# Experts' weights read in longer runs, the router tile by tile, and the first group of tokens gathered by a product

## The chip, the cores and the metric

One core of a Trainium2 chip runs the whole program. Its engines are TensorE (PE; its weight loads are PEld), VectorE (DVE), ScalarE (ACT), GpSimd (POOL) and SyncE (SP), and sixteen DMA engines move data. The metric is the device time of one execution in microseconds. All arithmetic is in f32.

## The reference

Three layers over 256 tokens of 1024 features. The first block has two (a gated-scan mixer and windowed attention, each followed by an MLP); the second block has one layer that ends in a mixture of experts, which is where most of the change lies:

```python
x = x + g1[:, None, :] * mix
h2 = _rms(x, norm2_g[l]) * (1.0 + sc2[:, None, :]) + sh2[:, None, :]
g_logits = hf @ w_rg + b_rg                      # 4 groups
e_logits = (hf @ w_re + b_re).reshape(-1, 4, 4)  # 16 experts
...                                              # best group, its best 2 experts, softmax weights
for e in range(N_EXPERTS):                       # 16 experts, 1024 -> 512 -> 1024
    he = jax.nn.silu(hf @ w1[e]) * (hf @ w3[e])
    y = y + combine[:, e:e + 1] * (he @ w2[e])
x = x + g2[:, None, :] * y
```

Each of the 256 tokens takes two experts, so 512 pairs are spread over 16 experts, unevenly.

## The kernel before

Each engine has an order of its own, written out by hand, and semaphores join them. SP issues all large weight loads in one fixed order. PSUM has eight banks; PE takes them in turn (`claim`) and other engines free them (`free`, `moved`).

The expert stage works on slots. Every expert has 64 slots (`SLOTS`); seven more units of 64 slots (`SPILLS`) take what overflows. So there are 23 units, in the order of `moe_order`: experts 0, 1, spill unit 0, experts 2, 3, spill unit 1, and so on to 12, 13, spill unit 6, 14, 15. Two units' slots make a group of 128 rows; there are 12 groups. A spill unit is computed whether or not it is needed, but its weights are loaded only where a table, made at run time, says that an expert overflowed.

What leads to the first unit, in order:

- DVE adds the last output projection to the residual, normalises both tiles of tokens (`rms_row`), PE transposes them (`turn_x("moe", ...)`), ACT and DVE apply scale and shift (`modulate`), PE makes the gate rows and the router's product for both tiles, and DVE picks experts with small operations.
- PE's product `pos` counts tokens per expert; DVE turns the counts into slots (`slot_i`, `slots_ready`).
- POOL scatters the token rows to their slots in DRAM (`x_slots`, four indirect DMAs, `x_spread`), loads the first group of 128 rows back (`load_group`), PE transposes it (`turn_group`), and ACT and DVE apply scale and shift (`modulate_group`, `hs_ready`).
- Meanwhile DVE makes `pick_late`, one-hot weights with which the last two units' results are added to tokens by PE instead of through DRAM; PE transposes them (`turn_picks`).

Then each unit is `up(i)`: 16 products of 64 slots by 512 columns of w1 and w3, in two pairs of 64 columns of the array, with `turn_he(i-1)` in their middle; `turn_group` where a group begins; and `down(i-1)`: 8 products with w2. ACT makes the silu and DVE the gated product `he`. DVE scales the result (`keep_y`) and POOL stores it to `y_slots`, from which four indirect loads at the end collect each token's two rows.

SP's order for the expert weights (`load_up`: w1 and w3, 2 MB each; `load_down`: w2, 2 MB): experts 0 and 1, spill unit 0 (after the table and the scatter, since its buffer lies over the token rows), then 2, 3 and so on. Two experts' buffers alternate, so `load_up(e)` waits until expert e-2 is through `up`. w1 and w3 are read as `(k p) n -> p k n`: partition p takes row k*128+p of each of 8 blocks, 2 KB at a time; w2's rows are 4 KB.

GpSimd's queue also carries, at the start of the second block, small loads (`rel_bias`, norm vectors, router weights `wr`), and inverse square roots for DVE (`inverse_roots`).

## Time and profile before

| | us |
|---|---|
| median of three runs (1716.3 to 1721.85) | 1717.02 |
| the profiled execution's own time | 1726.32 |
| its span, first to last instruction | 1724.5 |
| TensorE busy in the span (94%) | 1626.6 |
| VectorE busy (40%) | 697.5 |
| ScalarE busy (15%), GpSimd busy (6%) | 256.0, 108.3 |
| DMA moved in the span | 333.94 MB |

Read it as a stage at a time: a share over the whole span averages stages with different limits. The profiled execution took 9.3 us more than the median; sums below are made against the profiled one. "Issue" in the chain is time in which an engine waited for nothing that the profile can name, a weight load among it. A matmul in f32 shows as two records, a transpose as one. The DMA share can read over 1, since packets overlap.

### The profile page before, as it was taken

What the parts mean: (1) busy time and instruction counts of PE and PEld (TensorE: products, weight loads), DVE (VectorE), ACT (ScalarE), POOL (GpSimd) and SP (SyncE); (2) the same over time, 40 slices, a digit from 0 to 9 for tenths busy, and PEclk for the clock granted to TensorE, in tenths of its full rate; (3) what the DMA queues carried; (4) which work ended last, traced back from release to release, by engine and by line L of the source; (5) the groups of instructions that cost most, each with busy time, mean ns of one, the idle gap of its engine ahead of it and who ended that gap; (6) DMA issues with size and microseconds to landing.
All of it is one profiled execution on the core that took longest, in us unless ns stands there. A gap on an engine that the chain in (4) does not pass through costs nothing.

```text
span 1724.5 us, 17356 instructions
## 1 busy us (share of the span) xinstructions
PE 1626.6 (94%) x6960; PEld 878.5 (51%) x6960; DVE 697.5 (40%) x1322; ACT 256.0 (15%) x576; POOL 108.3 (6%) x123
## 2 busy tenths in 40 slices
PE   4999999999999999999989999999989958998997
PEld 2445556474444444446756788448855633333332
DVE  1617853468886000112264765004484342111112
ACT  3121113010000000000154110000222311011110
POOL 1000001100000000001000100001131110110101
PEclk9999999999999999999989999999999978999999
DMA  9452441146665321107610699424623449999996
GB/s 340 169 195 99 146 165 56 49 147 219 214 225 207 135 98 49 49 1 257 225 50 1 229 333 363 175 98 154 197 98 122 147 178 354 390 392 391 391 387 254
DMA packets 160623, 333.94 MB, mean 194 GB/s; under 512 B 15288, under 2 KB 15568, under 8 KB 160544
## 3 DMA queue, kind: packets, MB, share of 16 engines
q1 hardware_dynamic: 141408, 298.90, 47.7%
q0 software_dynamic: 18224, 30.78, 5.5%
q10 hardware_dynamic: 912, 3.17, 0.5%
q8 instruction: 55, 0.90, 0.2%
q14 instruction: 24, 0.20, 0.0%
HBM read 355.02 MB, written 15.48 MB: 215 GB/s over the span
## 4 chain that ended last, share of the span: by engine, by line
PE 88%; DMA 4%; DVE 4%; issue 2%; POOL 1%; ACT 1%; SPq 0%; DVEq 0%; ACTq 0%; POOLq 0%
PE psum L624 85%; PE psum L628 4%; DMA wring<-in_ev_w_in 2%; DMA wring<-in_w_mod 1%; DMA wring<-in_mlp_w 1%; ACT wide L1663 0%; POOL small L1523 0%; DVE wide L2068 0%; DVE big L2401 0%; DMA x_slots<-wide,slot_i 0%; DVE big L2560 0%; DMA big<-x_slots 0%; DVE small L2559 0%; POOL x_slots L1609 0%; DVE small L2183 0%
## 5 line engine op out<-in xcount | busy, mean ns | idle before, releaser
L624 PE MATMUL psum<-wring,big 128*128 128x512 f32 (+2 forms) x1600 | 559.6, 579 | 13.8 <-issue 13.3
L624 PE MATMUL psum<-wide,wring 128*128 128x256 f32 (+3 forms) x1872 | 490.2, 437 | 0.2
L624 PEld LDWEIGHTS psum<-wring,big 128*128 128x128 f32 (+1 forms) x1600 | 242.8, 173 | 310.1 <-issue 306.1
L624 PEld LDWEIGHTS psum<-wide,wring 128*128 128x128 f32 (+1 forms) x1872 | 304.3, 184 | 173.0 <-issue 144.6
L624 PE MATMUL psum<-wring,wide 128*128 128x512 f32 (+3 forms) x576 | 216.1, 576 | 9.0 <-DMA wring<-in_w_mod 5.4
L1663 ACT ACTIVATE big<-psum 128x512 f32<-128x512 f32 (+2 forms) x155 | 83.0, 546 | 665.0 <-PE psum L624 614.3
L2068 DVE SCALAR_TENSOR_TENSOR wide<-wring,csilu,wide 128x512 f32<-128x512 f32 x252 | 175.5, 748 | 3.0
L624 PEld LDWEIGHTS psum<-wring,wide 128*128 128x128 f32 (+1 forms) x576 | 97.7, 188 | 109.2 <-issue 96.0
L2168 DVE TENSOR_TENSOR wide<-psum,gate 128x512 f32<-128x512 f32 x27 | 18.7, 691 | 325.2 <-PE psum L624 325.0
L1523 POOL TENSOR_TENSOR small<-small 128x1 f32<-128x1 f32 (+2 forms) x30 | 41.1, 1372 | 1037.8 <-DVE small L2185 884.7
L1663 ACT ACTIVATE wide<-psum 128x256 f32<-128x256 f32 (+2 forms) x114 | 46.0, 418 | 313.3 <-PE psum L628 158.9
L624 PE MATMUL psum<-big,wide 128*64 128x512 f32 (+1 forms) x408 | 90.7, 566 | 0.0
L2836 DVE TENSOR_TENSOR wide<-wide,psum 128x256 f32<-128x256 f32 x23 | 9.7, 421 | 179.0 <-ACT wide L1663 179.0
L2068 DVE SCALAR_TENSOR_TENSOR big<-wring,csilu,big 128x512 f32<-128x512 f32 x112 | 74.9, 745 | 0.0
L2216 DVE TENSOR_TENSOR big<-big,psum 128x512 f32<-128x512 f32 (+1 forms) x62 | 35.1, 567 | 97.3 <-ACT big L1663 94.3
L1663 ACT ACTIVATE wide<-psum,modc 128x256 f32<-128x256 f32 (+1 forms) x36 | 16.2, 514 | 348.8 <-PE psum L628 348.6
L624 PE MATMUL psum<-big 128*64 128x128 f32 (+5 forms) x592 | 59.3, 328 | 7.7 <-ACT wide L1663 3.6
L624 PEld LDWEIGHTS psum<-big,wide 128*64 128x64 f32 (+1 forms) x408 | 30.8, 142 | 49.2 <-issue 48.3
L624 PE MATMUL psum<-wide,lnb 128*64 128x512 f32 x224 | 50.8, 595 | 0.0
L624 PEld LDWEIGHTS psum<-big 64*128 64x128 f32 (+2 forms) x592 | 41.6, 168 | 17.1 <-issue 15.6
L628 PEld LDWEIGHTS psum<-const,wide 128*128 128x128 f32 x214 | 24.9, 150 | 37.9 <-issue 25.5
L628 PE MATMUL psum<-const,wide 128*128 128x128 f32 x214 | 35.3, 300 | 5.6 <-DVE wide L2208 4.8
(266 smaller groups left out, 885.5 us busy)
## 6 DMA issues: line engine op xcount, KB each, us to landing
wring<-in_mlp_w SPq DMA_DIRECT2D x32, 2048.0 KB, 8.7
wring<-in_w SPq DMA_DIRECT2D x32, 2048.0 KB, 21.9
wring<-in_w_mod SPq DMA_DIRECT2D x24, 2048.0 KB, 13.0
big<-in_w SPq DMA_DIRECT2D x23, 2048.0 KB, 20.6
wide<-in_w SPq DMA_DIRECT2D x14, 2048.0 KB
wring<-in_w_ada SPq DMA_DIRECT2D x12, 2048.0 KB, 8.6
wring<-in_w_in SPq DMA_DIRECT2D x8, 2048.0 KB, 8.4
wring<-in_ev_w_in SPq DMA_DIRECT2D x6, 2048.0 KB, 13.0
```

The lines of the kernel that those rows point to most:

```text
L624: return nc.tensor.matmul(o, a, b, start=first, stop=last)
L628: return nc.tensor.transpose(o, a, ident[0:n, 0:n])
L1523: nc.gpsimd.tensor_tensor(a, a, half_neg[:, 0:a.shape[1]], ALU.pow).then_inc(rate_done, 1)
L1663: return nc.scalar.activation(o, a, func, **kw)
L2068: ins = v_.scalar_tensor_tensor(acc, w, by, acc, ALU.mult, ALU.add)
L2168: free(v_.tensor_tensor(ubuf, bank(name), gate[:, gv, cs], ALU.mult), name)
L2216: free(v_.tensor_tensor(h, h, src, ALU.mult), name)
L2836: v_.tensor_tensor(he[:, i % 2, :], sg[:, i % 2, :], psum[:, i % 2, T:2 * T], ALU.mult).then_inc(he_ready, 1)
```

## The change

Four parts.

1. The experts' matrices are read with each partition taking neighbouring rows. w1 and w3 are read as `(p k) n -> p k n`: partition p takes rows 8p to 8p+7, one run of 16 KB. w2 is read as two halves of which partition p takes two neighbouring rows, runs of 8 KB. The inner dimension of a product is then dealt otherwise over partitions, so the token rows (`rms_row(t, True)`), the router's weights, the scale and shift (`modp`) and `he` are dealt the same way. `modp` comes from `modc` by way of DRAM: two stores of 1024 single numbers and one load, all in POOL's queue.
2. The router runs tile by tile: transposes, scale and shift, and product of tile 0 stand inside and right behind the output projection of tile 1. The gate rows come after both products.
3. The first group isn't read back from DRAM: DVE makes a one-hot matrix from the slots (`first_hot`) and PE multiplies the token rows with it (`gather_first`), which gives the transposed group. The scatter stays, for the other eleven groups.
4. `turn_picks` comes after `up(0)`, and the work of DVE and ACT around it is put in another order. The loads of spill unit 0 also wait for the gather.

On PE, from the second tile's output projection to the second unit, this stands in a row before (`small,wide` is the router, `const,modc` the gate rows, `lnb,const` the counting, `const,gate` the picks, `const,big` the group's transposes, `wring,big 64x512` an `up`):

```order
L624 MATMUL psum<-wring,big 128x512 x24
L628 MATMUL psum<-const,wide 128x128 x16
L624 MATMUL psum<-const,modc 128x128 x8
L624 MATMUL psum<-small,wide 128x20 x16
L624 MATMUL psum<-lnb,const 128x32 x2
L628 MATMUL psum<-const,gate 128x128 x4
L628 MATMUL psum<-const,big 128x128 x8
L624 MATMUL psum<-wring,big 64x512 x24
L628 MATMUL psum<-const,wide 128x128 x2
```

and now:

```order
L642 MATMUL psum<-wring,big 128x512 x16
L646 MATMUL psum<-const,wide 128x128 x8
L642 MATMUL psum<-wring,big 128x512 x8
L642 MATMUL psum<-small,wide 128x20 x8
L646 MATMUL psum<-const,wide 128x128 x8
L642 MATMUL psum<-small,wide 128x20 x8
L642 MATMUL psum<-const,modc 128x128 x8
L642 MATMUL psum<-lnb,const 128x32 x2
L642 MATMUL psum<-lnb,wide 128x128 x16
L642 MATMUL psum<-wring,big 64x512 x16
L646 MATMUL psum<-const,gate 128x128 x4
L642 MATMUL psum<-wring,big 64x512 x8
```

The router's product is in two halves, the first of them right behind the output projection; the gate rows have moved behind both; the group's eight transposes are sixteen products `lnb,wide`; and the picks stand behind the first unit.

On DVE, from the slots to the first unit (`table_i` says which spill units are needed, `modc` or `modp` marks the scale and shift of a group, `64x512` begins the picks), before:

```order
L2784 CAST slot_i<-lnb 128x4
L2787 TENSOR_TENSOR lnb<-lnb,const 128x112
...
L2793 CAST table_i<-lnb 128x14
L2796 TENSOR_TENSOR small<-small 128x2x4
L2797 TENSOR_TENSOR small<-small 128x2
...
L2804 TENSOR_TENSOR small<-small 128x2
L2809 COPY gate<-gate 64x512 x2
L2814 TENSOR_SCALAR wide<-const,lnb,small 128x128
...
L2823 TENSOR_SCALAR big<-psum,modc 128x128 x4
L2836 TENSOR_TENSOR wide<-wide,psum 128x256 x2
```

and now:

```order
L2841 CAST slot_i<-lnb 128x4
L2842 TENSOR_SCALAR small<-lnb 128x4
L2844 TENSOR_SCALAR lnb<-const,small 128x128 x2
L2846 SCALAR_TENSOR_TENSOR lnb<-const,small,lnb 128x128 x2
L2851 TENSOR_TENSOR lnb<-lnb,const 128x112
...
L2857 CAST table_i<-lnb 128x14
L2862 TENSOR_SCALAR big<-psum,modp 128x128 x4
L2868 TENSOR_REDUCE small<-small 128x2
...
L2878 COPY gate<-gate 64x512 x2
L2883 TENSOR_SCALAR lnb<-const,lnb,small 128x128
...
L2897 TENSOR_TENSOR wide<-wide,psum 128x256 x2
```

Five operations for `first_hot` stand between the slots and the table; the group's scale and shift have moved ahead of the picks.

The diff, without the declarations and the places that repeat an edit shown:

```diff
--- before.py
+++ after.py
...
@@ -444,0 +449 @@
+        modp_scratch = nc.dram_tensor("modp_scratch", [2, D], F32, kind="Internal").ap()
...
@@ -592 +600,11 @@
-                 "moe": (2, 1, 0, 0, 2, 4)}
+                 "moea": (2, 1, 0, 0, 1, 4), "moeb": (2, 1, 0, P, 1, 4)}
+
+        def shift_of(part, k):
+
+            l, half, v = PARTS[part][:3]
+            return modp[:, 0, k:k + 1] if (l, half) == (2, 1) else modc[:, l, 24 * half + k, v:v + 1]
+
+        def scale_of(part, k):
+
+            l, half, v = PARTS[part][:3]
+            return modp[:, 1, k:k + 1] if (l, half) == (2, 1) else modc[:, l, 24 * half + 8 + k, v:v + 1]
@@ -1294,2 +1312 @@
-            out_project(2, yT2, (2,), turn_second)
-            out_project(2, yT2, (3,))
+            def turn_routed(part, t):
@@ -1297,6 +1314,7 @@
-            pe.wait_ge(xn_ready, 4)
-            turn_x("moe", xn, (0, 1))
-            gate_rows(2, 1)
-            wait_h("moe")
-            o = claim("router")
-            for t in range(2):
+                pe.wait_ge(xn_ready, 3 + t)
+                turn_x(part, xn, (t,))
+
+            def router(part, t):
+
+                wait_h(part)
+                o = claim(f"router{t}")
@@ -1304,2 +1322,9 @@
-                    last = mm(o[:, t * 20:(t + 1) * 20], hT[:, k, t * P:(t + 1) * P], wr[:, k, :], k == 0, k == KC - 1)
-            last.then_inc(bank_full, 1)
+                    last = mm(o[:, 0:20], hT[:, k, t * P:(t + 1) * P], wr[:, k, :], k == 0, k == KC - 1)
+                last.then_inc(bank_full, 1)
+
+            out_project(2, yT2, (2,), turn_second)
+            out_project(2, yT2, (3,), lambda: turn_routed("moea", 0))
+            router("moea", 0)
+            turn_routed("moeb", 1)
+            router("moeb", 1)
+            gate_rows(2, 1)
@@ -1318,3 +1343,2 @@
-                pe.wait_ge(xs_in[n % 2], 16 * (n // 2 + 1))
-                if n > 0:
-                    pe.wait_ge(hs_ready, 2 * n)
+                pe.wait_ge(xs_in[n % 2], 16 * (n // 2 + n % 2))
+                pe.wait_ge(hs_ready, 2 * n)
@@ -1324,0 +1349,9 @@
+            def gather_first():
+
+                pe.wait_ge(first_ready, 1)
+                for k in range(KC):
+                    for t in range(2):
+                        last = mm(psum[:, 4 + k // 4, (k % 4) * P:(k % 4 + 1) * P], xn[:, t, k * P:(k + 1) * P],
+                                  first_hot[:, t, :], t == 0, t == 1)
+                last.then_inc(xs_turned, 1)
+
@@ -1388,3 +1421 @@
-            turn_picks()
-            turn_group(GROUP_ORDER[0])
-            pe.wait_ge(late_ready, 1)
+            gather_first()
@@ -1392,0 +1424,4 @@
+                if i == 0:
+                    turn_picks()
+                if i == 2:
+                    pe.wait_ge(late_ready, 1)
@@ -1441,0 +1477,4 @@
+            def by_halves(w):
+
+                return w.rearrange("p (h c) n -> p h c n", h=2)
+
@@ -1449 +1488 @@
-                    sp.dma_start(w13_ring[e % 2][:, w], src[0, e].rearrange("(k p) n -> p k n", p=P)).then_inc(w13_in[e % 2], 16)
+                    sp.dma_start(w13_ring[e % 2][:, w], src[0, e].rearrange("(p k) n -> p k n", p=P)).then_inc(w13_in[e % 2], 16)
@@ -1456 +1495 @@
-                sp.dma_start(w2_ring[:, e % 2], I["w2_2"][0, e].rearrange("(f p) n -> p f n", p=P)).then_inc(w2_in[e % 2], 16)
+                sp.dma_start(by_halves(w2_ring[:, e % 2]), I["w2_2"][0, e].rearrange("(h p c) n -> p h c n", h=2, c=2)).then_inc(w2_in[e % 2], 16)
@@ -1461,0 +1501 @@
+                    sp.wait_ge(xs_turned, 1)
...
@@ -1555,0 +1596,4 @@
+            pool.wait_ge(modc_ready, 4)
+            for j in range(2):
+                pool.dma_start(modp_scratch[j].rearrange("(k p) -> p k", p=P), modc[:, 2, 24 + 8 * j:32 + 8 * j, 0],
+                               allow_slow_non_contiguous=True).then_inc(modp_out, 16)
@@ -1561,2 +1605,2 @@
-                (wr[:, :, 0:4], I["w_rg_2"][0].rearrange("(k p) n -> p k n", p=P)),
-                (wr[:, :, 4:20], I["w_re_2"][0].rearrange("(k p) n -> p k n", p=P)),
+                (wr[:, :, 0:4], I["w_rg_2"][0].rearrange("(p k) n -> p k n", p=P)),
+                (wr[:, :, 4:20], I["w_re_2"][0].rearrange("(p k) n -> p k n", p=P)),
@@ -1565,0 +1610,2 @@
+            pool.wait_ge(modp_out, 32)
+            pool.dma_start(modp[:, :, :], modp_scratch.rearrange("j (p k) -> p j k", p=P)).then_inc(modp_in, 16)
@@ -1620 +1666 @@
-            loaded = 0
+            loaded = 1
...
@@ -1978 +2026,2 @@
-            modulate("moe")
+            modulate("moea")
+            modulate("moeb")
...
@@ -1994,2 +2042,0 @@
-            act.wait_ge(pick_turned, 1)
-            f(late_T, psum[:, 7, :].rearrange("p (u t n) -> p u t n", u=LATE, t=2), ACT.Copy).then_inc(late_ready, 1)
@@ -2001,0 +2049,3 @@
+                if i == 0:
+                    act.wait_ge(pick_turned, 1)
+                    f(late_T, psum[:, 7, :].rearrange("p (u t n) -> p u t n", u=LATE, t=2), ACT.Copy).then_inc(late_ready, 1)
...
@@ -2208 +2259,4 @@
-                signal(v_.tensor_scalar(xn[:, t, :], x, lnr, None, ALU.mult), xn_ready)
+                dst = xn[:, t, :]
+                if dealt:
+                    dst, x = dst.rearrange("p (k q) -> p k q", k=KC), x.rearrange("p (q k) -> p k q", k=KC)
+                signal(v_.tensor_scalar(dst, x, lnr, None, ALU.mult), xn_ready)
@@ -2726,2 +2780,2 @@
-                rms_row(t)
-            modulate("moe")
+                rms_row(t, True)
+                modulate(("moea", "moeb")[t])
@@ -2729,4 +2783,4 @@
-            o = ready("router")
-            free(v_.tensor_tensor(lg, o[:, 0:40].rearrange("p (t e) -> p t e", t=2),
-                             brr.unsqueeze(1).to_broadcast([P, 2, 20]), ALU.add), "router")
-            dve.wait_ge(*moved("router"))
+            for t in range(2):
+                free(v_.tensor_tensor(lg[:, t, :], ready(f"router{t}")[:, 0:20], brr, ALU.add), f"router{t}")
+            for t in range(2):
+                dve.wait_ge(*moved(f"router{t}"))
@@ -2761,0 +2816,3 @@
+            rt_x4 = rt_exp.rearrange("p (t e) -> p t e", t=2)
+            step(v_.tensor_tensor(rt_x4[:, :, 0:4], lg[:, :, 0:4], each(rt_g), ALU.subtract))
+            signal(v_.tensor_tensor(rt_x4[:, :, 4], rt_2, rt_1, ALU.subtract), route_ready)
@@ -2784,0 +2842,7 @@
+            step(v_.tensor_scalar(first_slot, slot_f, float((NEXP - LATE) * SLOTS), None, ALU.add))
+            for t in range(2):
+                step(v_.tensor_scalar(first_hot[:, t, :], cst("late"), first_slot[:, 0, t:t + 1], None, ALU.is_equal))
+            for t in range(2):
+                last = v_.scalar_tensor_tensor(first_hot[:, t, :], cst("late"), first_slot[:, 1, t:t + 1], first_hot[:, t, :],
+                                               ALU.is_equal, ALU.add)
+            last.then_inc(first_ready, 1)
@@ -2795,3 +2859,8 @@
-            rt_x4 = rt_exp.rearrange("p (t e) -> p t e", t=2)
-            step(v_.tensor_tensor(rt_x4[:, :, 0:4], lg[:, :, 0:4], each(rt_g), ALU.subtract))
-            signal(v_.tensor_tensor(rt_x4[:, :, 4], rt_2, rt_1, ALU.subtract), route_ready)
+            def modulate_group(g):
+                dve.wait_ge(xs_turned, GROUP_AT[g] + 1)
+                for k in range(4, KC):
+                    last = v_.tensor_scalar(slots_of(g)[:, k, :], psum[:, 5, (k - 4) * P:(k - 3) * P], modp[:, 1, k:k + 1],
+                                            modp[:, 0, k:k + 1], ALU.mult, ALU.add)
+                last.then_inc(hs_ready, 1)
+
+            modulate_group(0)
...
@@ -2833 +2894,0 @@
-            modulate_group(0)
@@ -2836 +2897,3 @@
-                v_.tensor_tensor(he[:, i % 2, :], sg[:, i % 2, :], psum[:, i % 2, T:2 * T], ALU.mult).then_inc(he_ready, 1)
+                v_.tensor_tensor(he[:, i % 2, :].rearrange("p (c q) -> p c q", c=2),
+                                 sg[:, i % 2, :].rearrange("p (q c) -> p c q", c=2),
+                                 psum[:, i % 2, T:2 * T].rearrange("p (q c) -> p c q", c=2), ALU.mult).then_inc(he_ready, 1)
```

## Rows read from the trace of the kernel before

**Rows 1.** Page, section 2: GB/s of the core's DMA in forty slices.
```profile
GB/s 340 169 195 99 146 165 56 49 147 219 214 225 207 135 98 49 49 1 257 225 50 1 229 333 363 175 98 154 197 98 122 147 178 354 390 392 391 391 387 254
```

**Rows 2.** A window of the expert stage: us, busy us (x) per engine, PEclk, DMA share, GB/s.
```profile
1450.00:1500.00 50.00, 47.85 (x228) 16.65 (x228) 8.55 (x20) 7.57 (x20) 4.48 (x6) 1.00 1.05 388
```

**Rows 3.** Waits of TensorE's matmuls, expert stage: total us, times, longest.
```profile
PE psum L624 <- issue: 13.3, 7, 2.4
```

**Rows 4.** Chain that ended last, expert stage: start, length, what.
```profile
1433.15 12.00 PE psum L624 x48
...
1449.11 1.03 PE psum L628 x8
...
1476.53 2.15 issue
...
1541.93 10.59 PE psum L624 x48
```

**Rows 5.** The same chain ahead of the first expert.
```profile
1421.27 4.08 DMA x_slots<-wide,slot_i
...
1425.64 3.85 DMA big<-x_slots
...
1431.51 1.64 issue
```

**Rows 6.** SyncE's DMA issues: the spill unit's weights.
```profile
1427.04 1.02 SPq L1470 DMA_DIRECT2D wide<-in_w  x2
```

**Rows 7.** DMA queues from 1427 to 1700 us: packets, MB, share of time.
```profile
q1 hardware_dynamic: 38987, 93.86, 91.2%
q0 software_dynamic: 12488, 11.65, 13.0%
```

**Rows 8.** Windows of other stages, columns as in rows 2.
```profile
25.00:35.00 10.00, 6.50 (x56) 2.77 (x48) 0.42 (x3) 1.87 (x4) 0.00 (x0) 1.00 1.05 387
...
1373.00:1377.00 4.00, 4.00 (x10) 1.73 (x10) 0.00 (x0) 0.00 (x0) 0.00 (x0) 1.00 1.01 393
1405.00:1409.00 4.00, 1.63 (x11) 1.52 (x10) 1.85 (x11) 0.00 (x0) 0.00 (x0) 0.56 1.03 410
...
1396.00:1402.00 6.00, 6.00 (x28) 6.00 (x29) 1.99 (x4) 2.56 (x5) 0.00 (x0) 0.50 1.03 372
1402.00:1405.00 3.00, 3.00 (x30) 3.00 (x28) 0.00 (x0) 0.67 (x2) 0.00 (x0) 0.99 1.06 401
```

**Rows 9.** Timeline from the normalised tokens to the first expert's input.
```profile
1395.19 0.75 DVE L2208 TENSOR_SCALAR wide<-xres,small 128x1024 f32<-128x1024 f32 x1 [0.67 <-POOL small L1523]
...
1396.00 3.67 PE L628 MATMUL psum<-const,wide 128*128 128x128 f32 x16 [4.55 <-DVE wide L2208]
...
1399.47 3.18 PE L624 MATMUL psum<-const,modc 128*128 128x128 f32 x16
...
1402.49 4.15 PE L624 MATMUL psum<-small,wide 128*128 128x20 f32 x32
...
1416.33 0.17 DVE L2784 CAST slot_i<-lnb 128x4 int32<-128x4 f32 x1
...
1422.61 0.35 DVE L2814 TENSOR_SCALAR wide<-const,lnb,small 128x128 f32<-128x128 f32 x1
...
1431.55 1.36 DVE L2823 TENSOR_SCALAR big<-psum,modc 128x128 f32<-128x128 f32 x4 [5.10 <-PE psum L628]
```

**Rows 10.** GpSimd's timeline when the third layer begins.
```profile
1210.25 0.57 POOL L1523 TENSOR_TENSOR small<-small 128x1 f32<-128x1 f32 x1
...
1226.81 0.94 POOL L1578 DMA_DIRECT2D gate<-rel_scratch  x1 [4.98 <-DMA rel_scratch<-big]
```

**Rows 11.** TensorE's timeline there: the two index-key transposes.
```profile
1220.19 0.44 PE L628 MATMUL psum<-const,big 128*128 128x128 f32 x2
```

**Rows 12.** DMA issues there: operation xcount, KB, us to landing.
```profile
small<-in_w_re POOLq DMA_DIRECT2D x1, 64.0 KB, 3.0
```

**Rows 13.** VectorE's timeline at the end, one 128x1024 operation.
```profile
1713.18 1.28 DVE L2845 SCALAR_TENSOR_TENSOR xres<-wide,small,xres 128x1024 f32<-128x1024 f32 x1
```

More of the change, by code:

```diff
@@ L229, in build @@
         modrows = sb("modrows", [P, P])
+        modp = sb("modp", [P, 2, KC])
         slot_i = sb("slot_i", [P, 4], I32)
@@ L484, in build @@
         modc_ready = sem("modc_ready")
+        modp_out = sem("modp_out")
+        modp_in = sem("modp_in")
         gkw_ready = sem("gkw_ready")
@@ L1694, in modulate @@
                 act.wait_ge(modc_ready, done)
+                if (l, half) == (2, 1):
+                    act.wait_ge(modp_in, 16)
                 width, per = n * P, 4 // n
@@ L1701, in modulate @@
                         last = f(hT[:, k, at:at + width], bank(name)[:, j * width:(j + 1) * width], ACT.Identity,
-                                 bias=modc[:, l, 24 * half + k, v:v + 1], scale=modc[:, l, 24 * half + 8 + k, v:v + 1])
+                                 bias=shift_of(part, k), scale=scale_of(part, k))
                     free(last, name)
@@ L1986, in modulate_group @@
                     last = f(slots_of(g)[:, k, :], psum[:, 4, k * P:(k + 1) * P], ACT.Identity,
-                             bias=modc[:, 2, 24 + k, 0:1], scale=modc[:, 2, 32 + k, 0:1])
+                             bias=modp[:, 0, k:k + 1], scale=modp[:, 1, k:k + 1])
                 last.then_inc(hs_ready, 1)
@@ L2140, in modulate @@
                 l, half, v, at, n, done = PARTS[part]
+                if (l, half) == (2, 1):
+                    dve.wait_ge(modp_in, 16)
                 width, per = n * P, 4 // n
@@ L2147, in modulate @@
                         last = v_.tensor_scalar(hT[:, k, at:at + width], bank(name)[:, j * width:(j + 1) * width],
-                                                modc[:, l, 24 * half + 8 + k, v:v + 1],
-                                                modc[:, l, 24 * half + k, v:v + 1], ALU.mult, ALU.add)
+                                                scale_of(part, k), shift_of(part, k), ALU.mult, ALU.add)
                     free(last, name)
@@ L2818, in _ @@
             dve.sem_inc(pick_ready, 1)
-            def modulate_group(g):
-                dve.wait_ge(xs_turned, GROUP_AT[g] + 1)
-                for k in range(4, KC):
-                    last = v_.tensor_scalar(slots_of(g)[:, k, :], psum[:, 5, (k - 4) * P:(k - 3) * P], modc[:, 2, 32 + k, 0:1],
-                                            modc[:, 2, 24 + k, 0:1], ALU.mult, ALU.add)
-                last.then_inc(hs_ready, 1)
             def keep_y(i):
```

14 lines of the change are left out of this document (9 added, 5 removed).

## Prediction

> **What bounds the kernel now.** I read the page's slices first. In the last eight the DMA moves about 390 GB/s without a break [rows 1], in no earlier stretch so long. So the expert stage was read next. There both candidates are nearly full: TensorE is busy 47.85 of 50 us at full clock, and the DMA share is 1.05 at 388 GB/s [rows 2]. What decides is who waits. TensorE's matmuls waited seven times for 13.3 us in that stage, none over 2.4 us, with no engine named [rows 3]. The first of these, 1.64 us, is the scale and shift of the first group [rows 5]; the other six, 11.7 us, stand in front of an `up` whose weights had just come, the first at 1476.53 for expert 3, 2.15 us [rows 4]. A unit without a wait takes 10.59 us and 0.37 for the two transposes, 1.03 more where a group is transposed [rows 4]. So a stage that could run at TensorE's pace is held back a little by its weights, over its whole length. A faster TensorE would bring nothing there, an earlier start only what the transfers also gain.
>
> The head of the stage is a chain: slots at 1416.5 [rows 9], scatter until 1425.35, load until 1429.5, transposes, scale and shift, first product at 1433.15 [rows 4, 5]. TensorE is nearly idle through it. The transfer of spill unit 0 starts at 1427.04 behind the scatter [rows 6]; from there to 1700 the queues carry 93.86 MB of weights and 11.65 MB of rows [rows 7], and never pause.
>
> **The router, tile by tile.** Today: tokens ready at 1396.0, 16 transposes 3.67 us, gate rows until 1402.5, router 4.15 us until 1406.6 [rows 9]. In the changed order the last output product ends 1.03 us later, since eight transposes stand inside it [rows 4]. The normalising operation now reads every eighth element. Contiguous it takes 0.75 us [rows 9]; 1.28 us is a 128x1024 operation at one element a cycle [rows 13]; no row shows a stride of eight. Bounds: 0 and +1.5 us (2.3 us in all, two cycles an element, estimated from rows 13); I take 1.28, so +0.5. Tokens are ready at 1397.5. Then eight transposes (1.03 at full clock, 1.84 at half), scale and shift 1.4, half a router (2.1, or 3.2 at the gate rows' 0.2 us a record): 1402.1 to 1404.1. I take the middle, 1403.1: 3.5 us earlier. The gate rows fit behind it, in the 9 us in which DVE picks experts.
>
> On the stride the Trainium skill (SBUF — State Buffer, the note on cachelines under its port swizzle) says that SBUF is read in 16-byte lines, that two hits a line are needed for full rate, and that at most four f32 of stride are free. By that the operation costs more than 1.28 us; it gives no price, and no run here shows one.
>
> **The head.** Slots come at 1413.0. Scatter and the transfer of spill unit 0 move with them: 1423.5 instead of 1427.04. The new path to the first product: one small operation 0.2 and four of 0.35 [rows 9] with their gaps, 1.65 us; sixteen products, 32 records at the gate rows' 0.2 us, since TensorE has idled and runs at half clock, 6.4 us (half of it at full clock); scale and shift 1.6. First product at 1422.7, 10.4 us earlier. The gather ends at 1421.1, before the scatter at 1421.9, so the new wait of SP costs nothing; if the gather were over 0.8 us later, SP would wait, and all expert loads are queued behind it. DVE's picks (6 us of small operations) now run under `up(0)`, 7 us long. TensorE gets their four transposes, 0.5 us, into the busy stage. Because it has been busy for 6 us with the gather, `up(0)` should not start cold: it took 12.00 where others take 10.59 [rows 4], -1.4 us.
>
> **Longer runs.** Pure 2 KB runs move 387 GB/s at share 1.05. 4 KB runs (w2) move 393 in one stretch and 410 in another [rows 8]. Per run and engine 2 KB take 84.7 ns; 4 KB take 166.8 or 159.8. Continued as a fixed part and a part per byte, 16 KB gives 398 or 429 GB/s. No row shows a run over 4 KB, so below nothing must be held open too. I take 418 for the mix, nearer to the stretch with the fuller share. Today's mix of two 2 KB matrices and one of 4 KB is 394.
>
> **The sum, against the profiled execution.** Expert 3's weights land at 1478.68 behind 14.7 MB of weights since 1427. Transfers start 3.5 earlier; the first group's 0.52 MB is not in their way, 0.7 (half of its 1.35 us fell after 1427); 14.7 MB at 418 instead of 394, 2.1. So they land 6.3 us earlier, at 1472.4. TensorE gets there at 1476.5 - 10.4 - 1.4 + 0.5 = 1465.2, and waits 7 us. The head's gain is thus mostly turned into a longer wait. That wait is long enough to lose the clock: after 4.55 us of idleness before 1396.0 the granted clock was 0.50 (1.2 GHz) for six us of work, and 0.99 after [rows 8, 9]. Six us at half clock lose 3.0. From there on the other five waits, 9.5 us, have to be paid off: 69.2 MB of weights follow until the last wait, at 418 they take 10.1 us less. So these waits go; for what is left of them I keep 0.5. Sum: -6.3 + 3.0 - 9.5 + 0.5 = -12.3 us. The tail stays: last unit, the store of `y_slots`, four gathers. The profiled execution would be 1726.3 - 12.3 = 1714.0, and the median 1717.0 - 12.3 = 1704.7.
>
> **Edits at nothing.** `modp` puts two stores of 1024 single numbers and a wait for them into GpSimd's queue, ahead of eight small loads' end and of an inverse root that DVE takes at 1210.25 [rows 10]. A load of 1024 short runs lands in 3.0 us [rows 12]; a store to DRAM was waited for 5.0 us [rows 10]. With 1.9 us for the two issues, the root comes about 3 us later, and what hangs on it, two transposes at 1220.19 [rows 11], has 5.3 us of cover after DVE's 4.1 us of work. So nothing; up to 3 us if the stores land 5 us late among the weights. The strided `he` has 7 us of cover (a `down` and half an `up`). ScalarE's and VectorE's two waits for `modp` are long over.
>
> **A rule against the change.** The rows show 387 to 394 GB/s for 2 KB runs and 393 to 410 for 4 KB [rows 8]. The Trainium skill (DMA: Bandwidth & Descriptors, Specifications) puts the shortest run for line rate at 512 bytes; by it every load here is at line rate already, and part 1 brings nothing. The rate of 410 against 387 speaks against it, the 393 for it. It is the first rival.
>
> **Rivals.**
> - The rate stays (0.16). 393 for a w2 stretch speaks for it. All is then bound by the transfers, which only start earlier: -3.5 - 0.7 = -4.2, 1712.8. In the trace, waits in front of `up` all along.
> - The transfers stop binding altogether (0.12): head -10.4 - 1.4, all six waits -11.7, picks +0.5: -23.0, 1694.0. It needs expert 3 to come 7 us sooner than I have it, and over 429 GB/s.
> - Slower: long runs lower the rate (0.08). A DMA share of 1.03 with only 372 GB/s exists [rows 8], so full engines can deliver less; a 16 KB run holds an engine eight times as long, and row traffic waits behind it. 93.86 MB at 394 take 238 us, so each per cent costs 2.4 us; from 1.8% lower the change loses, from 3.9% by over 0.3%. At 372 it is 5.6%: +13.4 - 4.2 = +9.2, 1726.
> - The `modp` detour reaches TensorE (0.07): 3 us on top of the forecast, 1708.
>
> **How the numbers follow.** The forecast has 0.57; alone its range is 1699 to 1711 (rate 429 to 398, the clock kept or lost, the router at either end). About 0.3%, 5 us, is what a measurement of this kernel can tell from no change. Faster: 0.57 + 0.12 + 0.07 = 0.76. Same: 0.16. Slower: 0.08. The range of 1694 to 1715 leaves out the slower case and what lies under the third.
>
> **What would show it.** Right: GB/s of the last slices at 410 or more; the first product near 1423; one wait of about 7 us in front of expert 3, with the clock at 0.5 behind it; hardly any wait after. Wrong: rate under 400; six waits as before; a wait of TensorE near 1220; the first product after 1427, which would mean that the gather is dearer than 0.2 us a record.

## The result, and the profile after

The changed kernel takes 1752.36 us (median of 4 runs, 1744.36 to 1754.25), the kernel before 1718.57 beside it (4 runs): ratio 1.0176, interval 1.0142 to 1.0210. It is slower by about 30 us, where 12 us faster was forecast. The profiled execution took 1752.73 us with a span of 1750.9.

First the page's GB/s and its packets.

```profile
GB/s 342 160 192 96 145 171 46 57 160 192 244 189 252 85 96 74 22 1 340 165 18 49 287 333 319 144 48 193 202 96 73 149 297 418 417 305 399 331 376 136
DMA packets 125760, 333.45 MB, mean 190 GB/s; under 512 B 15352, under 2 KB 15648, under 8 KB 116976
```

Where the stream of weights ran at 387 to 392 in every slice of the last stage [rows 1], it now runs at 417 and 418 and then drops to 305 and 331. The higher rate was forecast (418). The holes were not. Windows of that stage, columns as in [rows 2]:

```profile
1450.00:1500.00 50.00, 46.80 (x216) 16.00 (x214) 6.49 (x15) 6.09 (x16) 4.33 (x6) 0.97 1.02 419
1500.00:1550.00 50.00, 34.63 (x152) 12.29 (x150) 5.18 (x13) 4.66 (x13) 3.58 (x5) 0.88 0.93 374
1550.00:1600.00 50.00, 50.00 (x234) 16.80 (x232) 6.24 (x14) 5.24 (x14) 4.37 (x6) 0.98 0.91 347
1600.00:1650.00 50.00, 41.58 (x192) 14.79 (x190) 6.67 (x15) 5.70 (x15) 4.40 (x6) 0.90 0.90 348
```

TensorE is busy 173 of 200 us here, and from 1500 us on the DMA share is under 1: neither is full, so something else is waited for. The waits from 1425 to 1750 us name it (total us, times, longest):

```profile
DVE lnb L2893 <- DMA y_slots<-lnb: 123.6, 13, 18.2
...
PE psum L646 <- DMA big<-x_slots: 23.6, 3, 8.4
```

L2893 is VectorE's gated copy of an expert's result into one of two buffers; before it may write, the store of two units ago must have landed. In the kernel before no such row existed, and TensorE had no waits between 1440 and 1690 us but those of [rows 3]. The second row is a group of tokens that TensorE turns late. The chain that ended last runs through the two transfers from its start (start, length, what):

```profile
1449.85 26.10 DMA y_slots<-lnb
...
1477.02 37.54 DMA y_slots<-lnb
...
1516.68 30.42 DMA big<-x_slots
...
1566.16 29.19 DMA y_slots<-lnb
```

From issue to landing a store of `y_slots` took 12.6 us before (median from 1440 us on) and takes this now:

```profile
DMA to landing us min/median/max: 8.6/25.7/37.5
```

Two buffers and a unit of 10.8 to 12.0 us cover some 22 us. So a store of 12.6 us is never seen, and one of 37 us stops VectorE, then TensorE, then, since rings are not freed, SyncE's next loads: that is the hole in the GB/s. Part of the loss is TensorE's clock. Between 1462 and 1630 us it was granted 0.50 (1.2 GHz) in four stretches of 27 us together, the three later ones beside waits of 6 to 8 us. TensorE was busy 14.7 us in them, so at most some 7 us went that way (an estimate, by half of that busy time). In the kernel before the clock stayed at 1.00 there. The group loads, in the same queue of GpSimd behind the stores, went from 14.5 to 28.9 us.

The head of the stage, by contrast, is as forecast (timeline: start, length, engine, line, instruction, idle before it):

```profile
1420.09 0.17 DVE L2841 CAST slot_i<-lnb 128x4 int32<-128x4 f32 x1
...
1421.91 5.42 PE L642 MATMUL psum<-lnb,wide 128*128 128x128 f32 x32 [5.31 <-DVE lnb L2846]
...
1428.99 7.09 PE L642 MATMUL psum<-wring,big 128*64 128x512 f32 x32 [1.66 <-ACT big L1709]
```

The whole stage begins 6.9 us later than in the profile of before (about 4 of it from `modp`, below, the rest from where the third layer starts, which differs between executions). With that taken off, the first product starts 11.1 us earlier than before.

### The profile page after: what moved, and what is told of

Its sections match the earlier page's. It is cut to its first block, busy times and chain, and to the rows that moved or that the text cites. A ratio compares the mean times of both kernels' runs of the same rounds, so it can differ in the third digit from the quotient of the medians.

```text
span 1750.9 us, 17425 instructions
## 1 busy us (share of the span) xinstructions
PE 1639.8 (94%) x6984; PEld 885.9 (51%) x6984; DVE 699.7 (40%) x1332; ACT 257.3 (15%) x580; POOL 110.4 (6%) x125
## 4 chain that ended last, share of the span: by engine, by line
PE 76%; DMA 15%; DVE 4%; issue 1%; POOL 1%; SPq 1%; ACT 1%; DVEq 0%; ACTq 0%; POOLq 0%
PE psum L642 73%; DMA y_slots<-lnb 7%; DMA big<-x_slots 5%; PE psum L646 3%; DMA wring<-in_w_mod 1%; DMA wring<-in_mlp_w 1%; SPq L1474 1%; DMA wring<-in_ev_w_in 1%; POOL small L1563 0%; ACT wide L1709 0%; DVE lnb L2893 0%; DVE wide L2118 0%; DVE big L2455 0%; DVE big L2614 0%; ACT big L1709 0%
## 5 line engine op out<-in xcount | busy, mean ns | idle before, releaser
L2219 DVE TENSOR_TENSOR wide<-psum,gate 128x512 f32<-128x512 f32 x27 | 18.7, 691 | 321.7 <-PE psum L642 321.5
L1709 ACT ACTIVATE wide<-psum 128x256 f32<-128x256 f32 (+2 forms) x114 | 46.1, 418 | 318.6 <-PE psum L646 163.7
L2893 DVE TENSOR_TENSOR lnb<-psum,gate 128x512 f32<-128x512 f32 x23 | 15.9, 692 | 154.0 <-DMA y_slots<-lnb 123.6
L646 PE MATMUL psum<-const,big 128*128 128x128 f32 (+1 forms) x204 | 30.6, 297 | 35.8 <-DMA big<-x_slots 23.6
L646 PEld LDWEIGHTS psum<-const,big 128*128 128x128 f32 (+1 forms) x204 | 24.7, 151 | 50.2 <-DMA big<-x_slots 26.2
```

The lines of the kernel that those rows point to most:

```text
L646: return nc.tensor.transpose(o, a, ident[0:n, 0:n])
L1709: return nc.scalar.activation(o, a, func, **kw)
L2219: free(v_.tensor_tensor(ubuf, bank(name), gate[:, gv, cs], ALU.mult), name)
L2893: v_.tensor_tensor(ysb[:, i % 2, :], psum[:, 6 + i % 2, :], gy, ALU.mult).then_inc(ysb_ready, 1)
```

## Experiments

First round: which part is it. Ratios are to runs of the kernel before on the same chip, with the 95% interval.

**Only the long runs**, added to the kernel before, w1/w3 as below, w2 in its halves, the spill units alike:

```diff
-sp.dma_start(w13_ring[e % 2][:, w], src[0, e].rearrange("(k p) n -> p k n", p=P))
+sp.dma_start(w13_ring[e % 2][:, w], src[0, e].rearrange("(p k) n -> p k n", p=P))
```

> The kernel before with the longer runs alone: w1 and w3 in 16 KB, w2 in 8 KB (the tokens and router are not dealt accordingly, so the experts' products are of other numbers). Theory A, row traffic of y_slots and x_slots waits behind the long runs: stores of y_slots land after 20 to 30 us instead of 12.6, VectorE waits for them, the stream reaches 415 GB/s when it runs, and the time is 25 to 35 us over before, about 1745. Theory B, the long runs are harmless and the loss lies in the new head or in the modp detour: the waits in front of up shrink and the time is 8 to 12 us under before. Theory C, long runs lower the rate itself: over before, with the stream under 390 GB/s.

Measured 1746.99, ratio 1.0162 (1.0120 to 1.0204). VectorE waited 128.3 us in 13 waits for `y_slots`. Window 1500 to 1550: TensorE busy 38.45, 322 GB/s. So this part carries the whole loss.

**The changed kernel with 2 and 4 KB runs**, the same lines the other way round.

> The changed kernel with its expert weights read in 2 and 4 KB runs again, all else kept (the experts' products are of other numbers). Theory A: stores land in 12 to 14 us, no wait of VectorE for them, six waits in front of up come back; head -4, modp +4: about 1717, no change against before. Theory B: stays near 1750.

1724.51, ratio 1.001 (0.999 to 1.003). The stores land in 12.9 us, VectorE doesn't wait for them; TensorE waits 17.3 us for weights. The earlier head is turned into waits when the stream is not faster.

**`modp` late**: its two stores and its load stand behind the inverse root for the index keys in GpSimd's queue; in the changed kernel the stores stand ahead of the third layer's small loads, and the load behind most of them.

```diff
 pool.wait_ge(x_ready, 12)
-pool.dma_start(modp_scratch..., modc...)   # two; behind the small loads a wait and modp<-modp_scratch
...
+pool.dma_start(modp_scratch..., modc...)   # the same three
 pool.wait_ge(kln_ready, 1)
```

> The changed kernel with the modp stores, their wait and the load moved in GpSimd's queue behind the loads of the output norm's vectors, where it idles for 27 us. The detour cost 4 us in the trace (index-key transposes at 1224.6 against 1220.2, of which 2.7 were there before, and 2.3 more until 1260). Expected 4 us under the changed kernel, about 1747; if the detour cost nothing, 1751. The waits for the stores of y_slots stay on either theory.

1742.3, ratio 1.0137 (1.0083 to 1.0192): 7 us less than the changed kernel by the ratios, with intervals that overlap. VectorE still waited 135.0 us for the stores.

**The head alone**: router by tile, gather and picks in the kernel before, `modc` as it was, old runs.

> The kernel before with the router tile by tile, the gather by a product and the picks behind the first unit, but the old dealing of rows, 2 and 4 KB runs and no modp. The transfers bound the stage and start 3 to 4 us earlier, so both theories give 4 us under before, about 1713; the first product comes 11 us earlier and the wait in front of expert 3 grows to about 8 us.

1717.58, ratio 0.9975 (0.9949 to 1.0000). TensorE waits 18.8 us for weights in 6 waits, the longest 11.4, in place of 13.3 in 7 [rows 3]. Most of the 10 us won at the head are paid back in front of expert 3, as forecast.

Second round: is it the length of a run, and by which way. All on the kernel with `modp` late.

**4 KB runs** and **8 KB runs**: each w1/w3 load cut into 4 or 2 DMAs, w2 into 2 or 1, so that a run of a partition is 4 or 8 KB.

```diff
-sp.dma_start(ring[:, w], src.rearrange("(p k) n -> p k n", p=P))
+for q in range(2):                          # 4 for runs of 4 KB
+    sp.dma_start(ring[:, w][:, q*4:(q+1)*4], src.rearrange("(q p k) n -> q p k n", q=2, p=P)[q])
```

> The changed kernel with the late modp detour and the same dealing of rows, but each weight matrix read by more DMAs so that every run is 4 KB (w1 and w3 four DMAs each, w2 two). Theory A (row traffic waits in proportion to the length of the weights' runs): stores of y_slots land after 12 to 16 us, VectorE does not wait for them, the stream runs at 400 to 410 GB/s and the time is 5 to 12 us under before. Theory D (the loss comes from the dealing of rows or from the loads being queued earlier, not from the length of a run): stores land after 20 us or more and the time stays near 1745.

> The same with 8 KB runs throughout (w1 and w3 two DMAs each, w2 one). Theory A: in between, stores land after 15 to 20 us, which is near the 24 us that two buffers give, so few waits; time between 5 us under before and 5 over. Theory D: as at 16 KB, near 1745.

4 KB: 1712.53, 0.9926 (0.9908 to 0.9943), 402 GB/s, stores land in 14.3 us. 8 KB: 1710.89, 0.9932 (0.9916 to 0.9949), 410 GB/s, stores in 20.3. With 8 KB VectorE does wait, but TensorE doesn't feel it; the waits of that kernel:

```profile
DVE lnb L2897 <- DMA y_slots<-lnb: 72.5, 11, 10.1
```

and TensorE was busy 199.7 of 200 us. The rate rises with the run and so does the landing: 12.6, 14.3, 20.3 and 25.7 us for 2/4, 4, 8 and 16/8 KB.

**Stores through ScalarE's hardware queue**, long runs otherwise as in the first experiment. This asked whether GpSimd's queue was served badly.

```diff
-pool.dma_start(y_slots[...], ysb[:, i % 2, :])
+act.dma_start(y_slots[...], ysb[:, i % 2, :])
```

> The kernel before with the long runs alone (its experts' products are of other numbers), and the stores of y_slots issued by ScalarE on its hardware queue instead of GpSimd's software queue, a few us later in the unit. If any queue's rows wait behind long runs: they land after 20 to 35 us again and the time is near 1747. If it is the software queue that loses: they land under 10 us, VectorE does not wait for them, and the time falls to 1725 or less.

1802.56, 1.0460 (1.0443 to 1.0478). A store issued at 1451.8 freed VectorE at 1489.8, 38 us later; VectorE waited 163.7 us. So another queue alone is no cure. But the store had also changed its shape, which I had not asked for. The single packets of ScalarE's queue are 128 of 2 KB a store, none smaller, never more than two in flight at a time (three for moments), with two completion records a store where each transfer in GpSimd's queue has 16: the store ran on two of the sixteen DMA engines, 64 packets on each. The first store's packets went from 1455.6 to 1488.9, 0.52 us for each packet of an engine: its own 0.084 and, the rest, about one weight packet, whose mean was 0.47 then. GpSimd's group loads, now alone in their queue, landed in 8.9 us where the first experiment had 26.8. So neither queue is served worse; what counts is how many packets one engine has to carry, and the third round comes back to it. The rest of the loss is a new chain: ScalarE waited for results to store and was late with the silu of the next unit (160.6 us behind VectorE's copies). I had not priced that.

**Four buffers** for the results instead of two.

```diff
-ysb = region(lnb_flat, 0, 2, 512)
+ysb = four such buffers, two of them in gate; every i % 2 of theirs becomes i % 4
```

> The changed kernel with the late modp detour and four buffers for the results instead of two, 16 and 8 KB runs kept. Theory A with its price on the path (VectorE's wait for the store two units back): landing stays at 20 to 37 us, but four units are 46 us, so the wait is gone; what stays are waits of TensorE for a group of tokens, some 15 to 25 us. Expected about 1720. If the stores' landing were only a companion of something else that slows TensorE, the time stays near 1745.

1737.77, 1.0085 (1.0055 to 1.0114). VectorE's waits are gone, but stores land in 30.0 us (44.5 at most), and the group loads behind them are now what TensorE waits for:

```profile
PE psum L651 <- DMA big<-x_slots: 33.7, 3, 17.5
```

More cover moves the wait and doesn't remove it.

**Each store as two, of half the columns**, with 8 KB runs.

```diff
-pool.dma_start(y_slots[rows].rearrange("s (n c) -> n s c", n=2), ysb[:, i % 2, :])
+for q in range(2):
+    pool.dma_start(<the same>[:, :, cq], ysb[:, i % 2, cq])   # cq: 256 of 512 columns
```

> The kernel of e6 (8 KB runs, late modp detour), with each store of y_slots issued as two DMAs of 1 KB runs instead of one of 2 KB runs: the same bytes in twice as many runs, 16 for each DMA engine instead of 8. Theory A, each run of row traffic waits for some four runs of weights: the stores land after 30 to 40 us instead of 20, VectorE's wait for them reaches TensorE, and the time is 20 to 40 us over e6. Theory E, a store waits once for what is queued ahead of it, whatever its number of runs: landing 20 to 23 us and the time of e6, within 3 us.

1718.84, 0.998 (0.9956 to 1.0003). The landing stayed at 18.7 us, so my theory, that each row of a store waits for a few weight runs, fell: twice as many rows, no longer wait. What had not changed, as the table of the third round shows, is the number of packets. (It still cost 8 us, at 398 GB/s in place of 410; why, I can't say.)

**8 KB runs with `modp` early, and again with `modp` late**, on one chip, to price `modp`.

> The kernel of e6 with the modp detour back in its place of the changed kernel, so the changed kernel with 8 KB runs as its one difference. By the stretch from the last norm's root to the first decayed keys, 56.4 and 56.9 us with the early detour against 49.7 to 52.9 with the late one or none, it is 4 to 7 us slower than e6, about 1716; if the detour is covered, as the prediction had it, it equals e6.

> The kernel of e6 once more, beside e10 on the same chip: 0.7% under before again, 12 to 14 us; TensorE's waits in the expert stage stay under 6 us in all.

1715.63, 0.9966 (0.9946 to 0.9986), and 1710.62, 0.9944 (0.9921 to 0.9967). GpSimd in the first of them:

```profile
1205.62 0.54 POOL L1567 TENSOR_TENSOR small<-small 128x1 f32<-128x1 f32 x1 [3.03 <-DVE small L2262]
1206.12 2.20 POOL L1602 DMA_DIRECT2D modp_scratch<-modc  x2
...
1216.68 0.71 POOL L1615 DMA_DIRECT2D modp<-modp_scratch  x1 [2.36 <-DMA modp_scratch<-modc]
...
1218.22 0.57 POOL L1567 TENSOR_TENSOR small<-small 128x1 f32<-128x1 f32 x1
```

and in the second:

```profile
1197.12 0.55 POOL L1567 TENSOR_TENSOR small<-small 128x1 f32<-128x1 f32 x1 [3.04 <-DVE small L2262]
...
1204.56 0.57 POOL L1567 TENSOR_TENSOR small<-small 128x1 f32<-128x1 f32 x1
```

From the last root of the norm (the first row of each) to the root for the index keys it takes 12.6 us with the detour, 7.4 without; the difference of the median times is 5.0, with twelve runs of each, though the intervals of the ratios still touch.

Third round: what a store is made of. **Half of every store**: 64 rows of 2 KB, in the kernel of the first experiment.

```diff
-pool.dma_start(y_slots[rows].rearrange("s (n c) -> n s c", n=2), ysb[:, i % 2, :])
+pool.dma_start(y_slots[rows, 0:512], ysb[0:SLOTS, i % 2, :])
```

> The 16/8 KB runs alone (as e1_long_only, 1.0162 of before), but every store of y_slots moves only half its bytes: 64 rows of 2 KB, 128 KB, where e1's moves 128 of them. The other half of each result is left out (zeros, written once in the second layer, stand there). The small packets of the queue (9616 up to 512 B for 19 stores in e1, so a 2 KB row travels as four of about 512 B) fall to half per store; SyncE's weights are the same. Theory A (each small packet waits behind long weight packets, so the landing goes with the number of small packets): the store lands after about half of e1's 25 us median and 37 us maximum, 13 and 19 us; two buffers then suffice, VectorE's wait for y_slots falls from 128 us to under 30; the group loads wait less behind the stores in the same queue. Time 1700 to 1725 against 1725 of before (ratio 0.986 to 1.0), about 1715. Theory B (a long run delays each store by a fixed time, whatever its size): landing stays at 25 median and 37 at most, VectorE waits as long, ratio 1.016. Theory C (the group loads are the root): stores land sooner but TensorE's wait for x_slots takes the place as with four buffers, ratio 1.008.

1706.87, 0.9928 (0.9899 to 0.9958); one execution of ten took 8147 us, which I can't explain and the ratio leaves out. The store landed in 6.7 us, not in 13: far below theory A. And the small packets of the queue were gone. Queues from 1500 to 1560 us, first the changed kernel, then this one:

```profile
DMA packets 4570, 20.66 MB, mean 344 GB/s; under 512 B 2405, under 2 KB 2405, under 8 KB 2963
...
q0 software_dynamic: 2829, 2.30, 12.4%
```

```profile
DMA packets 2556, 24.72 MB, mean 412 GB/s; under 512 B 300, under 2 KB 300, under 8 KB 827
...
q0 software_dynamic: 655, 2.16, 9.0%
```

I had taken the small ones for 512 bytes. The single packets of the trace say otherwise. GpSimd's queue from 1440 us to the end, by recorded size (a few records are missing in the second row):

| kernel | 4 KB | 16 B | 8 B | 4 B |
|---|---|---|---|---|
| before, changed | 3008 | 0 | 9408 | 544 |
| 8 KB runs, four buffers | 2998, 3006 | 0 | 9300, 9379 | 544 |
| store as two of half the columns | 3008 | 9408 | 0 | 880 |
| half of every store, 64 rows | 2336 | 0 | 0 | 544 |

9408 by 21 stores is 448 packets of 8 bytes a store, beside 64 of 4 KB that already carry its 256 KB. They take 9 to 11 ns each, 2% of the engines' time. The 4-byte ones are 16 a DMA, one for each engine: its completion record. Bytes and packets were both changed by this experiment, so four more told them apart.

**The whole store as two of 64 rows**, in the kernel with `modp` late, then in the changed kernel with nothing else altered, then in the kernel before:

```diff
-pool.dma_start(y_slots[rows].rearrange("s (n c) -> n s c", n=2), ysb[:, i % 2, :])
+for h in range(2):
+    pool.dma_start(y_slots[rows, h * 512:(h + 1) * 512], ysb[h * SLOTS:(h + 1) * SLOTS, i % 2, :])
```

> e3_modp_late (16/8 KB runs, router by tile, gather, modp late; 1.0137 of before) with each store of y_slots written as two, of 64 rows by 2 KB each (partitions 0 to 63 into the left halves of the rows, 64 to 127 into the right), where one store took 128 partitions through a view of three dimensions. Every byte is stored. Theory P (packets): a store now is about 128 packets of 2 KB instead of 512 of 512 bytes, so it lands in about 10 us (e12, half of it: 6.7) instead of 20 to 37; VectorE's wait for y_slots falls from 135 us to under 10, the group loads land in 10 to 13 us; TensorE is full from 1450 to 1650; time 1690 to 1705, 0.981 to 0.990 of before, 8 to 20 us under the 8 KB runs. Theory B (bytes): landing 25 to 37 as before, time as e3, 1.014.

> The changed kernel with nothing altered but the stores of y_slots, as in e13. Theory P: about 5 us over e13 for the early modp stores, 1695 to 1710, 0.985 to 0.993 of before; that is 45 us less than the changed kernel, and near what was predicted for it. Theory B: 1.018 of before.

> The kernel before with nothing altered but the stores of y_slots, as in e13. Its VectorE never waited for the stores (landing 12.6 us), so there is no wait to remove. Theory P: the engines are spared 384 small packets a store; at 12.0% of the engines' time for 10.09 MB where 9.57 MB took 10.0% in e12, about 1 to 2% more is left for the weights: TensorE's waits of 13 us fall to about 9; 0.996 to 1.0 of before. Theory B: 1.0.

**Half of every store again, but by the view of three dimensions** (128 partitions, 256 columns).

> e12_half_stores with the half of the bytes taken otherwise: 128 partitions of 1 KB through the view of three dimensions (the left 256 of each partition's 512 columns), so about 256 small packets a store instead of about 64. The other half of each result is left out. Theory P: the store lands after about half of e1's 25 us median, 12 to 16 us, and not after 6.7; VectorE waits for it little or not (two buffers cover 23 us), so the time is near e12's 0.993 to 1.0. Theory B: 6.7 us as in e12.

| kernel | us | ratio (interval) | 8 or 16 B packets a store | store lands | group lands |
|---|---|---|---|---|---|
| long runs, `modp` late, two stores | 1703.80 | 0.9887 (0.9859 to 0.9915) | 0 | 6.3 | 10.7 |
| changed kernel, two stores | 1706.47 | 0.9898 (0.9873 to 0.9923) | 0 | 6.3 | 10.7 |
| before, two stores | 1715.43 | 0.9947 (0.9918 to 0.9976) | 0 | 5.3 | 7.1 |
| half, small packets | 1711.91 | 0.9910 (0.9880 to 0.9940) | 224 | 14.6 | 17.5 |

The landings came as theory P has them in all four, theory B's in none. Two of its times were short of the range: 0.9947 where 0.996 to 1.0 was expected for the kernel before, 0.991 where 0.993 to 1.0 was for the last. The changed kernel with its stores in another form takes some 48 us less by the ratios, 2.7% of itself. Its GB/s and windows:

```profile
GB/s 335 180 198 99 149 140 83 15 145 259 167 265 164 196 50 98 50 1 179 259 99 2 127 344 351 241 148 36 272 131 93 93 221 295 425 425 424 427 426 217
```

```profile
1450.00:1500.00 50.00, 46.24 (x219) 16.02 (x218) 7.26 (x17) 6.13 (x17) 5.35 (x10) 1.00 1.01 426
1500.00:1550.00 50.00, 50.00 (x238) 17.25 (x236) 8.22 (x18) 6.07 (x16) 5.83 (x11) 1.00 1.02 426
1550.00:1600.00 50.00, 50.00 (x242) 17.58 (x240) 8.55 (x20) 7.96 (x21) 6.51 (x13) 1.00 1.01 424
1600.00:1650.00 50.00, 50.00 (x240) 17.34 (x238) 7.61 (x17) 6.45 (x17) 4.80 (x9) 1.00 1.01 426
```

No hole is left, and TensorE's matmuls wait for weights twice in the whole stage:

```profile
PE psum L642 <- issue: 3.8, 2, 2.9
```

The fourth row of the table is the half store again with half the small packets, and it lands in 14.6 us where the same bytes without them land in 6.7. That made the small packets look like the cause, but the view was there with them and gone with them each time. The times of the single packets say what each does. Here are two stores, the first from the kernel before, with nothing else in GpSimd's queue, the second from the changed kernel, with a group load behind it (us):

| | before | changed |
|---|---|---|
| store issued | 1671.36 | 1449.85 |
| its first packet | 1675.60 | 1454.03 |
| the last of its 448 small packets | 1678.84 | 1472.88 |
| starts of 4 KB packets, some of 64 | 1676.13, .17, .36, .41, .60, .65 | 1454.16, .23, .92, .99, 1455.69, .75 |
| so one on each of two engines every | 0.24 | 0.76 |
| of that its own time, and the rest | 0.16, 0.08 | 0.16, 0.60 |
| the store has landed | 1683.66 | 1475.95 |

The 64 packets of 4 KB, all of the store's data, come in two strict rows, never more than two in flight: this form lies on two engines of sixteen, 32 packets on each. The 448 small ones are 14 times 32, so they are what the other fourteen engines get, and they are done 3 to 5 us before the store is. (The number of an engine isn't in the trace. It is read from the spacing, and from the completion records: in the first store fourteen come by 1678.94, the last two at 1683.17 and 1683.23.) The rest of each spacing is one weight packet, of 2 KB in this stretch of the kernel before, of 16 KB in that of the changed one. So an engine takes one packet of each queue in turn. With two stores of 64 rows each transfer has 32 packets of 4 KB, up to 14 of a pair's 64 were seen in flight at once, and 32 are two for each of sixteen engines.

The landings follow from this with nothing fitted. The first packet starts about 4 us after the issue; then each packet of the engine with the most costs its own 0.16 us and the mean weight packet of that kernel:

| | weight packet | packets an engine | gives | measured |
|---|---|---|---|---|
| before | 0.105 | 32 | 12.5 | 12.6 |
| 4 KB runs | 0.164 | 32 | 14.4 | 14.3 |
| 8 KB runs | 0.318 | 32 | 19.3 | 20.3 |
| 16/8 KB runs | 0.48 | 32 | 24.5 | 25.7 |
| half, through the view | 0.47 | 16 | 14.1 | 14.6 |
| two stores, 16/8 KB runs | 0.47 | 2 | 5.3 | 6.3 |
| two stores, kernel before | 0.10 | 2 | 4.5 | 5.3 |
| ScalarE's queue (own time 0.084) | 0.47 | 64 | 39 | 38 |

The sizes agree to about 1 us in all eight. It also says why the group loads suffered and why four buffers were no cure. Every engine has 32 packets of each store in GpSimd's queue, small or large, and each waits for a weight packet of 0.48 us: 15 us on fourteen engines, 20 on two, for a unit of 11. The queue falls behind for as long as the stream runs. With 8 KB runs the same is 10 us on fourteen and 15 on two.

The best version is the first of the table: the changed kernel, `modp` late, two stores of 64 rows; 1.1% under the kernel before.

## Why the prediction was wrong

**The step that failed** stands in the rival of the slower case: "a 16 KB run holds an engine eight times as long, and row traffic waits behind it". It was seen, and then priced as a lower rate alone (1726), and in the sum as nothing. It should have been a term of its own: a store needs 12.6 us, about 22 are covered, and its packets each wait for a weight packet. What the runs showed in its place: landings of 25.7 us in the median and 37.5 at most, 123.6 us of VectorE's waits, and a loss of 1.6% from the long runs alone. I never asked for the number of the packets in GpSimd's queue. [Rows 7] held it: 12488 packets for 11.65 MB are 933 bytes a packet, where its rows are of 2 and 4 KB. They are 780 an engine. With one weight packet each, of 0.48 us (the prediction's own run times give 0.46 to 0.49 for the mix), that is some 375 us of queue in a window of 273; with 8 KB runs it is 250. That the store lay on two engines no row of mine would have told.

With that wait taken away (the changed kernel with two stores) the ratio is 0.9898, 17.5 us under 1717.0; forecast were 12.3. That is not a confirmation, since the new form of the store alone brought 0.9947. Against the kernel before with two stores the rest of the change is worth 0.9898 / 0.9947 = 0.9951, some 8 us, and with `modp` late 0.9940, some 10 us, each with about 0.4% of uncertainty.

**The rate.** Forecast 418 from 398 to 429; the changed kernel ran at 417 to 419 wherever it was not stopped, 426 with the stores in the other form. Right. The 394 that I set against it was too high, though: it took w2's runs at 410, and [rows 1] show 387 to 392 for the mix, so the gain of the transfers was priced low. The Trainium skill's rule (DMA: Bandwidth & Descriptors, Specifications: from 512 bytes a run, line rate), the first rival, fell: 388 GB/s at 2 and 4 KB, 402 at 4, 410 at 8, 418 at 16 and 8.

**Router and head.** Forecast -3.5 for the slots, measured -3.1 (1420.09 against 1416.33 [rows 9] and the shift of 6.9); the second tile's half router took 3.57 us where at most 3.2 were allowed. Gather 6.4, measured 5.42. First product -10.4, measured -11.1. The strided operation 1.28, measured 1.15 us where a contiguous one takes 0.75 [rows 9]. The Trainium skill's note on cachelines (SBUF — State Buffer) has a stride of more than four f32 pay, and so it did, 1.15 against 0.75; that this meant more than 1.28 was my reading, and the trace disagrees with it. `up(0)` took 7.09 for 32 products, warm, as forecast.

**Expert 3.** A wait of 7 us was forecast, and 3 us of clock lost behind it. The head alone, at the old rate, waited 11.4 at most. With long runs and two stores the two waits for weights are 2.9 and 0.9 us, and the granted clock in 1450 to 1500 stays 1.00: no 3 us lost. The transfers gained a little more than I gave them.

**The other waits.** -9.5 + 0.5: confirmed where the stores don't interfere, none is left over 0.9 us.

**`modp`.** Forecast: root 3 us late, cover 5.3, cost nothing; a rival of up to 3 us had 0.07. The wait for the stores was 4.00 us in the changed kernel, and the root came 6.8 us later after the norm than before (14.25 against 7.42), past the cover. Measured 5.0 us with 8 KB runs, 2.7 with two stores, where the intervals overlap. The row I bounded it by, a landing of 3.0 [rows 12], was a load; these two stores of single numbers landed in 9.4 and 10.6 us, and behind them the load of that row took 12.1.

```profile
1218.27 0.71 POOL L1611 DMA_DIRECT2D modp<-modp_scratch  x1 [4.00 <-DMA modp_scratch<-modc]
...
1219.82 0.57 POOL L1563 TENSOR_TENSOR small<-small 128x1 f32<-128x1 f32 x1
```

**The tail** was not left alone in the end: the last store before the gathers cost GpSimd 8.7 us of waiting in the kernel before, 8.3 in the changed one, 5.4 in the kernel before with two stores and 2.2 in the changed one with two.

## What to carry to other kernels

Before a bulk stream is given longer runs, list the small transfers that share its engines, with each one's landing, its buffers' cover and above all its number of packets on the engine that has most of them: each of those waits for one packet of the stream, whatever its size. Compare bytes per packet of each queue with the row that you meant to move, and count how many of a transfer's packets are in flight at once; where the first is small or the second is two, write the transfer in another form first. An operation that is hidden today, with 12.6 us under a cover of 22, has a price as soon as its neighbour changes.

## What the hardware showed that I had not expected

A store from 128 partitions into a DRAM view of three dimensions (2 x 64 rows of 2 KB) puts its 64 packets of 4 KB on two engines and 448 packets of 8 bytes on the others; through ScalarE's queue the same view gives 64 packets of 2 KB on each of two engines and no small ones. Two stores of 64 partitions into plain rows use all sixteen and land in 5.3 instead of 12.6 us. That the outer size of 2 of the view sets the number of engines is likely; no run here varied it.

The other form helps even where nothing waited for a store: the kernel before gained 0.53% (I expected up to 0.4). TensorE's waits for weights fell from 13.3 us to 6.1, the rate rose from 388 to 396 and 401.

With 2 KB runs SyncE's own issue of a load blocks, with long runs it doesn't; the issues of one ring, before and after (ns min/median/max):

```profile
L1449 SPq DMA_DIRECT2D wring<-in_w x28: 378/4256/11715, 1441.7 to 1672.0; - x28
```

```profile
L1488 SPq DMA_DIRECT2D wring<-in_w x26: 327/394/608, 1444.2 to 1685.0; - x26
```
